# Decoder layer on one core: the samples' matrix states kept compact and turned by 64x64 products

## The chip, the cores and the metric

The kernel runs on one core of one Trainium2 chip. The metric is the device time of one execution in microseconds. The times of the kernel before are from three executions: 2606.88, 2611.5 and 2612.71 us, median 2611.5 us.

## The reference

One inference step of one layer of a hybrid decoder, for one prompt of 256 tokens and for 8 samples of 4 tokens each, all with 2048 channels. The layer normalises its input, projects it, and runs two branches side by side: a gated linear recurrence over channels, and an RWKV-7 branch with 32 heads of 64 channels. Each head has a 64x64 matrix state S (value x key). Both branches are projected back, merged, and followed by a squared-ReLU MLP and an embedding. What the change touches is the RWKV-7 state of the samples:

```
state_rwkv (DEPTH, DEC_BATCH, N_HEADS, HEAD, HEAD)   # 8 samples, 32 heads, [value, key]
sa = einsum('bhij,bhj->bhi', S, -kk_t)
S  = S * w_t[:, :, None, :] + sa[..., None] * b_t[:, :, None, :] + v_t[..., None] * k_t[:, :, None, :]
y  = einsum('bhij,bhj->bhi', S, r_t)
```

For the samples the kernel needs each state with its key index on the partitions, so every loaded 64x64 state is transposed once.

## The kernel before, in words

TensorE carries nearly everything. The large projections are cut into units: a unit is one 128-column slice of a weight against all 288 (or 296) token columns, 16 steps over the channels, three products each (high and low half of an fp32 number in two fp32r parts: `xh,wh`, `xl,wh`, `xh,wl`). SyncE loads the raw weight slice, ScalarE writes its high half `wh`, VectorE its low half `wl`, and TensorE multiplies.

The first half of the program is a loop of 16 steps, one per 128 channels, that is per pair of heads (the two heads are the two halves of 64 partitions, `head_rows(0)` and `head_rows(1)`). A step has six units, and each unit is cut into 8 slots, so a step has 48 slots. After the piece of a unit that belongs to a slot, every engine does the small stages that two tables (`EARLY` and `LATE`, line 137) put at that slot. `EARLY` belongs to the present pair of heads, `LATE` to the pair before. The order on each engine is thus written out by hand; between engines only semaphores order. Steps 0 and 1 are unrolled, steps 2 to 15 are a hardware loop, and the `LATE` stages of the last pair run beside the units of the gate projection that follows (called the last step below). What comes after (rest of the gate projection, output projections, MLP, embedding) has none of these stages.

The `LATE` stages that matter here:

- `state_in` (slot 11, lines 813 and 1168): TensorE turns the 8 sample states. The states of the two heads of a sample lie in `s0[:, b, :]` as a block-diagonal 128x128 tile whose other two blocks are zero (GpSimd clears `s0` once at the start, line 1908, first of six clears counted by `N_INIT`). `turn` (line 651) is a 128x128 transpose against the identity. The 8 results fill banks 2 and 3, and ScalarE copies each bank, 128x512, into `ms` (line 1171).
- `invert1a` to `invert5b` (slots 9 to 26): the blocks of the prompt's triangular inverse, in products of 32x32. An `a` part is 16 products into bank 6, which ScalarE copies into `yy` (line 1167); a `b` part is 16 or 32 products, which VectorE adds into `inv`. `invert2a` is at slot 12, `invert2b`, which needs the copy of `invert2a`, at slot 14.
- `samp_pair` (slot 15) writes bank 2 again and so waits for `state_read`; `samp_r` (slot 23) multiplies the turned states with `aex`, `samp_out` (slot 28) with `dg`: in both, 16 products of 64x64 with 64 columns, head 0 on rows and columns 0 to 63 of the array, head 1 on 64 to 127, by turns.
- `lowrank`, an `EARLY` stage at slot 8, writes bank 3, which ScalarE reads; the wait of `state_in` for `sig_ready` guards bank 3 against that.

SyncE loads the two heads of the next pair's states at unit 4 of a step (line 441), after the wait for `state_mm` of the pair before. `apart` (line 625) computes the value of a wait in a register ahead of the wait, where it depends on the loop counter.

All products go through one helper line (623), all transposes through line 652, so the trace tells them apart by the names of their tiles. An fp32 product has two records in the trace, a transpose one.

Of the kernel before, what the change touches and what calls it, by code (L numbers as in the profile page):

```python
# [69 lines left out]
def constants():  # L70
# [45 lines left out]

STEPS = {"dve_rg": 40, "dve_ch": 36}
ROW_LOADS = 27
N_INIT = 6
FFN_PLAN = (("up", 0), ("up", 1), ("down", 0), ("up", 2), ("down", 1), ("up", 3), ("down", 2), ("down", 3))  # L120


# [19 lines left out]
    6: ["rg_root"],  # L142
    9: ["invert1a"],
    10: ["invert1b", "rg_scan"],
    11: ["state_in"],
    12: ["invert2a"],
    14: ["invert2b"],
    15: ["samp_pair"],
    16: ["invert3a"],
# [23 lines left out]
def program(nc, a):  # L173
    ctx = ExitStack()
    with ctx:
# [31 lines left out]
        with mix:  # L207
            def mb(name, shape, dt=F32):
                return sb(name, shape, dt, mix)

            ptu, ptc = mb("ptu", [P, NPAR]), mb("ptc", [P, NPAR])
            dtc, dl = mb("dtc", [P, NDER]), mb("dl", [P, NCH])
            ex = mb("ex", [P, NX])
            zr, zk, zv = mb("zr", [P, NT]), mb("zk", [P, NT]), mb("zv", [P, NT])
            low = mb("low", [P, 4, NT])
            w2s, a2s, g2s = mb("w2s", [P, P]), mb("a2s", [P, P]), mb("g2s", [P, 2, P])
            was, wxs = mb("was", [P, P]), mb("wxs", [P, P])
            ue, xc, gg, gat = mb("ue", [P, 315]), mb("xc", [P, NT]), mb("gg", [P, NT]), mb("gat", [P, NT])
            rgi, th = mb("rgi", [P, NT]), mb("th", [P, NT])
            siga, sigw, gout, kp = (mb(n, [P, NT]) for n in ("siga", "sigw", "gout", "kp"))  # L220
            rn, ksq, kkn, bv = (mb(n, [P, NT]) for n in ("rn", "ksq", "kkn", "bv"))
            cum = mb("cum", [P, 5 * NB + NCH * (CHUNK + 1)])
            zeros = mb("zeros", [P, CHUNK])
            ar, btk = mb("ar", [P, 2, NT]), mb("btk", [P, 2, NT])
            btl, ktl = btk[:, 0, :], btk[:, 1, :]
            bkh, vv = mb("bkh", [P, 2, 2 * SAMP]), mb("vv", [P, 2, 2 * SAMP])
            tmb, tmv = mb("tmb", [P, 4, P]), mb("tmv", [P, 2, P])
            skv, suv, yts = mb("skv", [P, 2, HEAD]), mb("suv", [P, HEAD]), mb("yts", [P, HEAD])
            sbk, vpad = skv[:, 0, :], skv[:, 1, :]


            both = mb("both", [P, 9 * 4 * CHUNK])
            ams = both[:, 0:16 * CHUNK].rearrange("p (q t) -> p q t", q=4)
            am = both[:, 16 * CHUNK:16 * CHUNK + 16 * BLK].rearrange("p (l q t) -> p l q t", l=4, q=4)
            ab, yy = mb("ab", [P, 4, CHUNK]), mb("yy", [P, 4, BLK])
            inv, tt = mb("inv", [P, 8 * BLK]), mb("tt", [P, 4, CHUNK])
            tb, tn = (inv[:, k * 4 * BLK:(k + 1) * 4 * BLK].rearrange("p (q t) -> p q t", q=4) for k in range(2))
            sam, sq2, syy = mb("sam", [P, 4, SAMP]), mb("sq2", [P, 2, 2 * SAMP]), mb("syy", [P, SAMP])
            s0, ms = mb("s0", [P, NB, P]), mb("ms", [P, NB, P])
            aex, bke = mb("aex", [P, NB, 2, SAMP]), mb("bke", [P, NB, HEAD])  # L240

            dg = mb("dg", [P, NB, HEAD])
            so = dg
            rs, us, sr = mb("rs", [P, P]), mb("us", [P, P]), mb("sr", [P, HEAD])
            mp, mtmp = [mb(f"mp{k}", [P, P]) for k in range(2)], mb("mtmp", [P, P])
            sfin = mtmp
            yf, yc, ysq, sd = (mb(n, [P, NT]) for n in ("yf", "yc", "ysq", "sd"))
            dif, rgr, m2 = sd, yf, ysq
            rows = both[:, 0:D]
# [121 lines left out]
        def _(sp):  # L371
# [54 lines left out]
            def small(it, again):  # L426

                if again:
                    sp.wait_ge(cst_in, 16)
                    sp.wait_ge(bonus_mm, it)  # L430
                cols = bass.ds(it * P, P)
                sp.dma_start(g2s[:], a["rw_g2"][0, :, cols].rearrange("(k p) c -> p k c", p=P)).then_inc(small_in, 16)
                sp.dma_start(was[:], a["rg_wa"][0, bass.ds(it, 1)].rearrange("o c d -> (o c) d")).then_inc(small_in, 16)
                sp.dma_start(wxs[:], a["rg_wx"][0, bass.ds(it, 1)].rearrange("o c d -> (o c) d")).then_inc(small_in, 16)
                if again:
                    sp.wait_ge(cst_in, 16)
                    sp.wait_ge(state_mm, it)
                else:
                    sp.wait_ge(init_done, N_INIT)
                for h in range(2):  # L440
                    sp.dma_start(s0[h * HEAD:(h + 1) * HEAD, :, h * HEAD:(h + 1) * HEAD],
                                 a["state_rwkv"][0, :, bass.ds(2 * it + h, 1)].rearrange("b o i j -> (o i) b j")
                                 ).then_inc(s0_in, 16)

# [176 lines left out]
        def _(pe):  # L621
# [3 lines left out]
            def apart(value):  # L625


                if not isinstance(value, int):
                    value = pe.snap(value)
                    pe.compute_val(value)  # L630
                    pe.wait_ge(cst_in, 16)
                return value
# [18 lines left out]
            def turn(out, in_):  # L651
                return pe.transpose(out, in_, ident)  # L652
# [68 lines left out]
            def stage(name, p, last, four):  # L721
# [89 lines left out]
                                    done = mm(to(rb, 128, q), yy[rb, q, :], tn[rb, q, :], True, True)  # L811
                        done.then_inc(tn_mm, 1)
                elif name == "state_in":
                    pe.wait_ge(s0_in, 32 * one)
                    pe.wait_ge(ab_read, 2 * one)
                    if not last:
                        pe.wait_ge(sig_ready, 2 * one + 2)
                    for b in range(NB):
                        done = turn(bank[2 + b // 4][:, (b % 4) * P:(b % 4 + 1) * P], s0[:, b, :])
                    done.then_inc(state_mm, 1)  # L820
                elif name == "samp_pair":
                    count = apart(2 * one)
                    pe.wait_ge(state_read, count)
                    for h in range(2):
                        rows_h = head_rows(h)
# [20 lines left out]
                elif name == "samp_r":  # L846
# [3 lines left out]
                    for b in range(NB):  # L850
                        for h in range(2):
                            rows_h = head_rows(h)
                            mm(bank[3][rows_h, 0:HEAD], aex[rows_h, b, :, :].rearrange("p f t -> p (f t)"), ms[rows_h, b, rows_h], b == 0, False)
                    for h in range(2):
                        rows_h, rows_r = head_rows(h), slice(h * HEAD, h * HEAD + SAMP)
                        done = mm(bank[3][rows_r, 0:HEAD], sam[rows_h, 0, :], vpad[rows_h, :], False, False)
# [9 lines left out]
                elif name == "samp_out":  # L866
# [8 lines left out]
                    for b in range(NB):  # L875
                        for h in range(2):
                            rows_h = head_rows(h)
                            mm(bank[2][rows_h, b * HEAD:(b + 1) * HEAD], ms[rows_h, b, rows_h], dg[rows_h, b, :], b == 0, False)
                    for h in range(2):
                        rows_h = head_rows(h)  # L880
                        done = mm(bank[2][rows_h, :], suv[rows_h, :], bke[rows_h, :, :], False, True)
# [180 lines left out]
        def _(act):  # L1062
# [71 lines left out]
            def stage(name, p):  # L1134
# [32 lines left out]
                    act.activation(yy[:].rearrange("p a b -> p (a b)"), bank[6][:, 256:256 + 4 * BLK], ACT.Copy).then_inc(yy_read[int(name[6]) - 1], 1)  # L1167
                elif name == "state_in":
                    act.wait_ge(state_mm, one)
                    for b in range(2):  # L1170
                        act.activation(ms[:, 4 * b:4 * b + 4, :].rearrange("p a b -> p (a b)"), bank[2 + b][:], ACT.Copy).then_inc(state_read, 1)
                elif name == "samp_inv_a":
                    act.wait_ge(syy_mm, one)
                    act.activation(syy[:], bank[3][:, 0:SAMP], ACT.Copy).then_inc(syy_read, 1)
# [727 lines left out]
        @block.gpsimd  # L1902
        def _(pool):
            pool.memset(rows[0:NPAR, :], 0.0).then_inc(rows_zero, 1)

            pool.wait_ge(par_ready, 2)
            pool.wait_ge(nrm_lo, 8)
            for view, value in ((s0[:], 0.0), (cum[:], 1.0), (zeros[:], 0.0), (ue[:], 0.0), (sq2[:], 0.0), (vv[:], 0.0)):
                pool.memset(view, value).then_inc(init_done, 1)

            def samples(p):


                pool.wait_ge(am_ready, p + 1)
                if not (isinstance(p, int) and p == 0):
                    pool.wait_ge(so_saved, 16 * p)
                pool.tensor_tensor(aex[:], ar[:, :, samp_all].unsqueeze(1).to_broadcast([P, NB, 2, SAMP]),
                                   cst[:, C_SEQ:C_SEQ + 256].rearrange("p (b t) -> p b t", b=NB).unsqueeze(2).to_broadcast([P, NB, 2, SAMP]), ALU.mult)
                pool.tensor_tensor(dg[:], cst[:, C_ID2:C_ID2 + HEAD].unsqueeze(1).to_broadcast([P, NB, HEAD]),
                                   cum[:, NS * NB:(NS + 1) * NB].unsqueeze(2).to_broadcast([P, NB, HEAD]), ALU.mult)  # L1920
                pool.wait_ge(turn_read, p + 1)
                ins = pool.tensor_tensor(bke[:], sbk.unsqueeze(1).to_broadcast([P, NB, HEAD]),
                                         cst[:, C_SQT:C_SQT + NB].unsqueeze(2).to_broadcast([P, NB, HEAD]), ALU.mult)
                ins.then_inc(sexp_ready, 1)

            samples(0)
            with pool.Fori(1, KT) as p:
                samples(p)
# [30 lines left out]
```

## Time and profile before

| what | us |
|---|---|
| median of three executions | 2611.5 |
| the profiled execution | 2610.33 |
| span of its profile | 2608.6 |
| TensorE busy in the span | 2527.0 (97%) |
| VectorE busy | 1550.0 (59%) |
| ScalarE busy | 1114.7 (43%) |
| GpSimd busy | 62.8 (2%) |

The span is what the profile shows from the first to the last instruction; 1.7 us of the execution lie outside it. PE is TensorE's matmul side, PEld its weight loads, DVE VectorE, ACT ScalarE, POOL GpSimd. Matmuls overlap: the duration of one contains its way through the array, so the time that a block of them takes is read from the start of its first to the start of what follows it.

### The profile page before, as it was taken

How to read it: one execution, taken by the hardware profiler on the slowest of the kernel's cores; microseconds unless marked ns; L12 is line 12 of the kernel's file. 1: busy time of each engine (PE TensorE's matmuls, PEld its weight loads, DVE VectorE, ACT ScalarE, POOL GpSimd, SP SyncE). 2: the span in 40 equal slices, each digit the busy share in tenths (PEclk: the TensorE clock that was granted, in tenths of full speed). 3: DMA queues.
4: the chain of work that ended last, by engine and by line, in shares of the span. 5: the costliest groups of instructions: out<-in, count | busy, mean ns of one | idle time of the engine just before them, and what ended most of it. 6: DMA issues, size and time to landing. Idle time of an engine off the chain costs nothing.

```text
span 2608.6 us, 66543 instructions
## 1 busy us (share of the span) xinstructions
PE 2527.0 (97%) x27452; PEld 2368.5 (91%) x27452; DVE 1550.0 (59%) x2818; ACT 1114.7 (43%) x1514; POOL 62.8 (2%) x59
## 2 busy tenths in 40 slices
PE   5999999999999999998999999999999999999997
PEld 4988888888888888887999999999999999999996
DVE  5667776776676766774444566555444444446665
ACT  3545555555554544453433333444334324333333
POOL 0000000000000000000000000000000000000000
PEclk8999999999999999998999999999999999999998
DMA  5643434443434434343567665556655655665553
GB/s 159 156 109 101 113 93 115 103 109 100 113 97 115 115 99 115 97 111 96 138 188 224 184 184 161 162 164 167 168 161 163 175 161 161 168 166 164 158 152 93
DMA packets 699783, 363.59 MB, mean 139 GB/s; under 512 B 43905, under 2 KB 698531, under 8 KB 698659
## 3 DMA queue, kind: packets, MB, share of 16 engines
q1 hardware_dynamic: 699598, 360.70, 51.3%
q8 instruction: 168, 2.75, 0.5%
q14 instruction: 17, 0.14, 0.0%
HBM read 346.07 MB, written 14.59 MB: 138 GB/s over the span
## 4 chain that ended last, share of the span: by engine, by line
PE 90%; DVE 5%; DMA 1%; issue 1%; ACT 1%; DVEq 0%; SPq 0%; ACTq 0%
PE bank L623 89%; DVE sd L1710 1%; PE bank L652 1%; DVE yc L1380 1%; DMA raw<-w_in 1%; DVE wl L1722 1%; DVE nrm L1380 0%; ACT ysq L1197 0%; DMA gb_scratch<-gat 0%; DVE bv L1380 0%; DVE sd L1383 0%; DVE wl L1374 0%; ACT sd L1200 0%; DMA nsq<-ga_scratch 0%; DVE xl L1377 0%
## 5 line engine op out<-in xcount | busy, mean ns | idle before, releaser
L623 PE MATMUL bank<-xh,wh 128*128 128x288 f32 (+1 forms) x3136 | 1002.1, 320 | 17.8 <-DVE xl L1377 10.4
L623 PE MATMUL bank<-xh,wl 128*128 128x288 f32 (+1 forms) x3136 | 932.4, 297 | 0.9 <-issue 0.9
L623 PE MATMUL bank<-xl,wh 128*128 128x288 f32 (+1 forms) x3136 | 932.7, 297 | 0.0
L623 PEld LDWEIGHTS bank<-xh,wh 128*128 128x128 f32 x3136 | 593.9, 189 | 54.7 <-issue 16.3
L1374 DVE TENSOR_TENSOR wl<-raw,wh 128x2048 fp32r<-128x2048 f32 x206 | 472.1, 2292 | 232.5 <-ACT wh L1068 232.5
L623 PEld LDWEIGHTS bank<-xl,wh 128*128 128x128 f32 x3136 | 595.1, 190 | 6.0
L623 PEld LDWEIGHTS bank<-xh,wl 128*128 128x128 f32 x3136 | 594.5, 190 | 1.1 <-issue 1.1
L623 PE MATMUL bank<-sbh,wl 128*128 128x288 f32 x1792 | 534.0, 298 | 0.0
L623 PE MATMUL bank<-sbh,wh 128*128 128x288 f32 x1792 | 529.6, 296 | 1.8 <-DVE wl L1374 1.8
L623 PE MATMUL bank<-sbl,wh 128*128 128x288 f32 x1792 | 529.5, 295 | 0.0
L1068 ACT ACTIVATE wh<-raw 128x2048 fp32r<-128x2048 f32 x206 | 392.6, 1906 | 285.6 <-PE bank L623 276.4
L623 PEld LDWEIGHTS bank<-sbh,wh 128*128 128x128 f32 x1792 | 336.7, 188 | 2.1 <-issue 2.1
L623 PEld LDWEIGHTS bank<-sbl,wh 128*128 128x128 f32 x1792 | 338.4, 189 | 0.0
L623 PEld LDWEIGHTS bank<-sbh,wl 128*128 128x128 f32 x1792 | 336.7, 188 | 0.0
L1722 DVE TENSOR_TENSOR wl<-raw,wh 128x1024 fp32r<-128x1024 f32 x204 | 241.6, 1219 | 5.1 <-ACT wh L1234 4.2
L1234 ACT ACTIVATE wh<-raw 128x1024 fp32r<-128x1024 f32 x204 | 212.8, 1053 | 47.7 <-PE bank L623 47.3
L1329 ACT ACTIVATE tmp<-tmp 128x288 f32<-128x288 f32 x64 | 28.5, 445 | 225.3 <-DVE tmp L1380 225.3
L1377 DVE TENSOR_TENSOR rga<-rga,bank 128x288 f32 (+1 forms) x80 | 36.4, 454 | 145.1 <-PE bank L623 145.1
L1686 DVE COPY us<-bank 64x128 f32<-64x128 f32 x64 | 18.5, 289 | 141.8 <-PE bank L623 141.8
L1189 ACT ACTIVATE rs<-bank 64x128 f32<-64x128 f32 x64 | 17.4, 272 | 139.2 <-PE bank L623 139.2
L1377 DVE TENSOR_TENSOR sbl<-tmp,sbh 128x288 f32 (+1 forms) x64 | 29.3, 459 | 77.1 <-ACT sbh L1331 77.1
L1317 ACT ACTIVATE xh<-rga,par 128x288 fp32r<-128x288 f32 x32 | 17.2, 537 | 130.2 <-DVE rga L1377 130.2
(282 smaller groups left out, 2400.9 us busy)
## 6 DMA issues: line engine op xcount, KB each, us to landing
raw<-w_in SPq DMA_DIRECT2D x116, 1024.0 KB, 5.9
raw<-w_up SPq DMA_DIRECT2D x64, 1024.0 KB, 6.3
raw<-w_down SPq DMA_DIRECT2D x64, 1024.0 KB, 5.9
raw<-w_rg_o SPq DMA_DIRECT2D x16, 1024.0 KB, 6.0
raw<-w_rw_o SPq DMA_DIRECT2D x16, 1024.0 KB, 6.0
raw<-w_o SPq DMA_DIRECT2D x16, 1024.0 KB, 6.0
raw<-w_ple_gate SPq DMA_DIRECT2D x16, 1024.0 KB, 6.0
s<-state_rwkv SPq DMA_DIRECT2D x32, 128.0 KB, 4.2
```

The source lines that it names most:

```text
L623: return pe.matmul(out, lhsT, rhs, start=start, stop=stop, skip_group_check=True)
L652: return pe.transpose(out, in_, ident)
L1068: act.activation(wh[slot][:], raw[slot][:], ACT.Copy).then_inc(hi_done, 1)
L1189: act.activation(rs[rc, :], bank[4][rc, g * P:(g + 1) * P], ACT.Copy).then_inc(r_read[c], 1)
L1234: act.activation(wh[slot][:, k, :], raw[slot][:, k, :], ACT.Copy).then_inc((half_done, hi_done)[part], 1)
L1329: act.activation(tmp[u][:], tmp[u][:], ACT.Square).then_inc(h_sq, 1)
L1374: dve.tensor_tensor(wl[slot][:], raw[slot][:], wh[slot][:].bitcast(F32), ALU.subtract).then_inc(lo_done, 1)
L1377: return dve.tensor_tensor(out, x, y, op)
L1380: return dve.scalar_tensor_tensor(out, x, s, y, op0, op1)
L1686: dve.tensor_copy(us[rc, :], bank[5][rc, 0:P]).then_inc(u_read, 1)
L1710: dve.reciprocal(sd[:], sd[:]).then_inc(ch.sem, ch.one())
L1722: ins = dve.tensor_tensor(wl[slot][:, k, :], raw[slot][:, k, :], wh[slot][:, k, :].bitcast(F32), ALU.subtract)
```

## The change

The states are kept as 64 columns a sample instead of 128, with head 0 on partitions 0 to 63 and head 1 on 64 to 127 and no zero blocks. Each state is turned by a product with the 64x64 identity (`C_ID2` of the constants), which makes 16 products on 64x64 parts of the array instead of 8 transposes on the whole. The result is one bank (2) instead of two, copied once. The stage stands in slot 12 behind `invert2a` instead of in slot 11. The wait for `sig_ready` is gone since bank 3 is no longer written, and the other two waits take their values through `apart`. GpSimd's clear of `s0` is gone, so five clears are counted. The readers of `ms` address it without the head's column offset.

```diff
-N_INIT = 6
+N_INIT = 5
-    11: ["state_in"],
-    12: ["invert2a"],
+    12: ["invert2a", "state_in"],
-            s0, ms = mb("s0", [P, NB, P]), mb("ms", [P, NB, P])
+            s0, ms = mb("s0", [P, NB, HEAD]), mb("ms", [P, NB, HEAD])
@@ SyncE, small()
-                    sp.dma_start(s0[h * HEAD:(h + 1) * HEAD, :, h * HEAD:(h + 1) * HEAD],
+                    sp.dma_start(s0[h * HEAD:(h + 1) * HEAD, :, :],
@@ TensorE, state_in
-                    pe.wait_ge(s0_in, 32 * one)
-                    pe.wait_ge(ab_read, 2 * one)
-                    if not last:
-                        pe.wait_ge(sig_ready, 2 * one + 2)
+                    count = apart(32 * one)
+                    pe.wait_ge(s0_in, count)
+                    count = apart(2 * one)
+                    pe.wait_ge(ab_read, count)
                     for b in range(NB):
-                        done = turn(bank[2 + b // 4][:, (b % 4) * P:(b % 4 + 1) * P], s0[:, b, :])
+                        for h in range(2):
+                            rows_h = head_rows(h)
+                            done = mm(bank[2][rows_h, b * HEAD:(b + 1) * HEAD], s0[rows_h, b, :], cst[rows_h, C_ID2:C_ID2 + HEAD], True, True)
@@ TensorE, samp_pair
-                    count = apart(2 * one)
+                    count = apart(one)
                     pe.wait_ge(state_read, count)
@@ TensorE, samp_r (and in samp_out the same edit of ms)
-... ms[rows_h, b, rows_h] ...
+... ms[rows_h, b, :] ...
@@ ScalarE, state_in
-                    for b in range(2):
-                        act.activation(ms[:, 4 * b:4 * b + 4, :].rearrange("p a b -> p (a b)"), bank[2 + b][:], ACT.Copy).then_inc(state_read, 1)
+                    act.activation(ms[:].rearrange("p a b -> p (a b)"), bank[2][:], ACT.Copy).then_inc(state_read, 1)
@@ GpSimd
-            for view, value in ((s0[:], 0.0), (cum[:], 1.0), (zeros[:], 0.0), (ue[:], 0.0), (sq2[:], 0.0), (vv[:], 0.0)):
+            for view, value in ((cum[:], 1.0), (zeros[:], 0.0), (ue[:], 0.0), (sq2[:], 0.0), (vv[:], 0.0)):
```

## Rows read from the trace of the kernel before

**Rows 1.** The page, first part: busy time, share of the span, instructions.
```profile
PE 2527.0 (97%) x27452; PEld 2368.5 (91%) x27452; DVE 1550.0 (59%) x2818; ACT 1114.7 (43%) x1514; POOL 62.8 (2%) x59
```

**Rows 2.** TensorE's waits in the loop: total us, times, longest.
```profile
PE bank L623 <- ACT yy L1167: 7.4, 2, 4.1
PE bank L623 <- ACT rs L1189: 7.1, 16, 0.5
```

**Rows 3.** Timeline of TensorE, slots 11 and 12 of one step: start, length.
```profile
704.78 0.30 PE L623 MATMUL bank<-xh,wl 128*128 128x296 f32 x1
704.91 1.03 PE L652 MATMUL bank<-cst,s 128*128 128x128 f32 x8
705.71 0.38 PE L623 MATMUL bank<-xh,wh 128*128 128x296 f32 x1
705.92 0.29 PE L623 MATMUL bank<-xl,wh 128*128 128x296 f32 x1
...
706.47 0.30 PE L623 MATMUL bank<-xh,wl 128*128 128x296 f32 x1
706.70 0.45 PE L623 MATMUL bank<-inv,both 32*32 32x32 f32 x32
707.08 0.40 PE L623 MATMUL bank<-xh,wh 128*128 128x296 f32 x1
707.32 0.30 PE L623 MATMUL bank<-xl,wh 128*128 128x296 f32 x1
```

**Rows 4.** The chain of waits over the loop: start us, us, what.
```profile
634.70 0.87 PE bank L652 x8
...
705.08 0.87 PE bank L652 x8
...
1207.24 7.16 DMA gb_scratch<-gat
```

**Rows 5.** Timeline of TensorE, samp_out and r0 of the same step.
```profile
728.84 1.15 PE L623 MATMUL bank<-dg,ms 64*64 64x64 f32 x32
729.82 1.03 PE L623 MATMUL bank<-bke,suv 64*64 64x512 f32 x4
730.68 0.25 PE L623 MATMUL bank<-cst,yts 64*64 64x32 f32 x4
730.77 0.66 PE L623 MATMUL bank<-tmv,both 64*64 64x64 f32 x16
```

**Rows 6.** Timeline of TensorE, samp_u and invert5b, then my0.
```profile
726.17 0.33 PE L623 MATMUL bank<-sr,sq 32*64 32x64 f32 x4
726.43 0.21 PE L623 MATMUL bank<-yy,inv 32*32 32x32 f32 x1
...
734.51 0.33 PE L623 MATMUL bank<-us,tmb 64*64 64x64 f32 x4
734.68 0.28 PE L623 MATMUL bank<-tmv,tmb 64*64 64x64 f32 x4
734.79 0.33 PE L623 MATMUL bank<-both,us 64*64 64x64 f32 x4
```

**Rows 7.** Timeline of ScalarE, the same step.
```profile
705.99 1.09 ACT L1171 ACTIVATE ms<-bank 128x512 f32<-128x512 f32 x2 [1.48 <-PE bank L652]
...
707.53 1.28 ACT L1130 ACT_TABLE_LOAD   x1
...
711.61 0.45 ACT L1132 ACTIVATE rn<-rn 128x288 f32<-128x288 f32 x1 [1.04 <-DVE rn L1383]
```

**Rows 8.** Timelines of TensorE: a hiccup in the loop; the last step.
```profile
225.85 0.24 PE L623 MATMUL bank<-inv,both 32*32 32x32 f32 x2 [0.42 <-issue]
...
1216.08 0.65 PE L623 MATMUL bank<-yy,inv 32*32 32x32 f32 x32 [3.34 <-ACT yy L1167]
```

**Rows 9.** The states' tile s: the clear, and the load's issue-to-landing.
```profile
L1909 POOL MEMSET s<- x1: 955/955/955, 56.2 to 56.2; 128x1024 f32 x1
DMA to landing us min/median/max: 3.8/4.2/4.9
```

More of the change, by code:

```diff
@@ L852, in stage @@
                             rows_h = head_rows(h)
-                            mm(bank[3][rows_h, 0:HEAD], aex[rows_h, b, :, :].rearrange("p f t -> p (f t)"), ms[rows_h, b, rows_h], b == 0, False)
+                            mm(bank[3][rows_h, 0:HEAD], aex[rows_h, b, :, :].rearrange("p f t -> p (f t)"), ms[rows_h, b, :], b == 0, False)
                     for h in range(2):
@@ L877, in stage @@
                             rows_h = head_rows(h)
-                            mm(bank[2][rows_h, b * HEAD:(b + 1) * HEAD], ms[rows_h, b, rows_h], dg[rows_h, b, :], b == 0, False)
+                            mm(bank[2][rows_h, b * HEAD:(b + 1) * HEAD], ms[rows_h, b, :], dg[rows_h, b, :], b == 0, False)
                     for h in range(2):
```

## The prediction, made before the changed kernel was run

> **What bounds the kernel.** I read the page's first part first: TensorE is busy for 2527.0 of 2608.6 us, 97%, and no other engine reaches 60% [rows 1]. An edit pays only by what it takes off TensorE's queue, or by a wait of TensorE that it shortens. The second view was therefore TensorE's own waits in the loop of 16 steps. Two matter: 16 waits of at most 0.5 us for ScalarE's `rs` at slot 34, which `state_in` does not feed, and two long ones, together 7.4 us, for the copy `yy` [rows 2]. Both long ones lie in the last step, where ScalarE stands behind the store of a gate (below). In the 14 steps of the hardware loop TensorE goes through slots 9 to 28 nearly without a pause, so there a nanosecond of its work is a nanosecond of the run. A step takes 70.38 us, from one `state_in` to the next (634.70 to 705.08) [rows 4].
>
> The third view was the timeline of slots 11 and 12. From 705.92 to 706.47 there are four intervals between large products, 0.137 us each. The 8 transposes start at 704.91, the next large product at 705.71 and the one after at 705.92 [rows 3]. From 704.78 to 705.92 are 1.14 us, where two intervals of 0.137 would have stood: the transposes cost 0.87 us. The chain of waits gives the same figure, 0.87, for this step, and it has 15 such pieces at `state_in`'s place, one a step, all of 0.87, of which two stand in the rows; only the last step's is missing [rows 4].
>
> **The change, part by part.**
>
> *TensorE, removed:* 8 transposes and their place in slot 11, -0.87 us a step.
>
> *TensorE, added:* 16 fp32 products, each with 64 rows, 64 columns of weights and 64 moving columns, the heads by turns on opposite quarters of the array, 32 records. The trace has exactly this shape: the `dg,ms` block of `samp_out`. Its 32 records start at 728.84, and the next block of the same shape of array starts at 729.82 [rows 5]: 0.98 us, 31 ns a record. That a product accumulates there and starts afresh here is no difference that I price. Nearest rows on both sides: 4 records of `us,tmb` take 0.17 us, 42 ns each, and 4 of `tmv,tmb` 0.11 us, 27 ns each [rows 6]. Bounds for the block are so 0.88 and 1.36 us; I take 0.98, because that row is the same pattern at the same length.
>
> *TensorE, the company it keeps.* A block on parts of the array pays for the change of shape. Into `invert2a` the distance from start to start is 0.23 us instead of 0.14 (706.47, 706.70), and behind it the first large product takes 0.24 (707.08, 707.32) [rows 3]; the end of the block itself also hides a gap. Its size between small shapes: 4 records of 64x32 followed by the same shape of array take 0.09 us (730.68, 730.77) [rows 5], 4 records of 32x64 followed by 32x32 take 0.26 (726.17, 726.43) [rows 6]. The difference, 0.17 us, is what I charge for going from 32x32 to 64x64 inside slot 12. Entry from and return to the large shape are already paid by `invert2a`; that is what the new place saves. The bounds of this term: 0, if the change of shape hides behind the last 32x32 products, and 0.17.
>
> Sum for a step: -0.87 + 0.98 + 0.17 = +0.28 us. By the low bounds it is -0.87 + 0.88 + 0 = +0.01, by the high ones -0.87 + 1.36 + 0.17 = +0.66.
>
> The Trainium skill ("TensorEngine Tiling (Array Packing)", Performance Considerations, Instruction Overhead) says that each matmul bears about 60 cycles of overhead on this chip, which speaks against 16 short products in place of 8 long ones. If that were paid on top of the columns by each of the 32 records, it would be, as an estimate from that page at 2.4 GHz, 25 ns more a record and 0.8 us more a step. The `dg,ms` row, 31 ns a record in all, leaves no room for it; where it came from, some of it would be in the 42 ns of `us,tmb`.
>
> *How many steps count.* Fifteen: the unrolled first one, 14 in the loop. In the last step TensorE does not set the pace: the chain goes through a store of the gate, `gb_scratch<-gat`, from 1207.24 for 7.16 us [rows 4], and TensorE sits idle for 3.34 us until 1216.08 behind it [rows 8]. The store is released by VectorE, which waits for nothing of `state_in`, so 0.28 us more is swallowed there, and a cheaper `state_in` would not have helped either. Sum: 15 x 0.28 = +4.2 us; bounds +0.2 and +9.9.
>
> *The waits.* The states are issued in unit 4 of the step before and land in 4.2 us [rows 9], with more than 10 slots to spare before they are used. `ab_read` is done at slot 6. `sig_ready` gone: the transposes started 0.13 us behind the product before them [rows 3], so none of the three waits cost anything, and nothing is gained by dropping one. The two `apart` are instructions of TensorE's queue and not of its array. `invert2a`, which has one, enters 0.09 us late in all [rows 3], and most of that is the change of shape; for two behind 32 queued records I take zero, at most 0.09. Queued behind the new block's waits are the large products of slot 13, which wait for nothing more, since both semaphores rose several slots before.
>
> *ScalarE.* The copies took 1.09 us together, from 705.99 on [rows 7]; one takes half, 0.5 to 0.6. But it now comes after the `yy` copy. With slot 11 empty everything starts 0.87 earlier: `yy` is copied about 706.4 to 706.7, the turning ends about 707.3, the copy runs to about 707.95, and the table load that stood at 707.53 starts 0.4 us later. Behind it `rn` waits 1.04 us for VectorE anyway [rows 7], so the delay is swallowed. `invert2b` needs `yy` only at slot 14, 2 us on, and `samp_pair` needs the copy at slot 15, about 3 us later. Gain and cost zero. Without that cover, 0.4 us a step would be 6 us.
>
> *VectorE* does nothing for `state_in`. *SyncE* issues the same two loads with the same 256-byte pieces in memory; its wait for `state_mm` comes at unit 4, 20 slots after the turning: zero. *GpSimd* loses a clear of 0.96 us at 56.2 [rows 9]; those that ask for the clears do so in the first step's own slots, much later: zero, and 0.96 us at the most if one had waited. The readers of `ms` fetch the same 64 contiguous numbers: zero.
>
> The profiled execution took 2610.33 us and its span 2608.6; with 4.2 more, 2614.5 and 2612.8. Its time is 1.2 us under the median of the three, so for the median I predict 2611.5 + 4.2 = 2615.7, rounded to 2615.5 us. Three executions spread over 5.8 us, and about 0.2%, 5.2 us, is what can be told from no change.
>
> **The rivals.**
>
> *A. Each short product costs more than the twin row says* (slower). 32 weight loads of 64x64 in place of 8 of 128x128, each hidden only behind 64 columns. For it: the 42 ns of `us,tmb` [rows 6]. Against it: that is a block of four with nothing to pipeline, the long block shows 31. Price 15 x 0.66 = +9.9 us, 2621. It decides from +0.35 us a step (5.2 us over 15 steps): block and switch together over 1.22 us, or 33 ns a record with the switch at 0.17.
>
> *B. TensorE's instruction supply* (slower). The step gets 48 more instructions (64 loads and products for 16) in the densest part of the queue. In some steps TensorE already halts for 0.42 us in the middle of a block of 32x32 products with nothing but issue to blame, at 225.85 and in four other steps [rows 8]. If all 15 steps halt once, that is ten more halts, +4.2 on top of 4.2: 2620. Equally the boundary can move to a harmless place, which takes back 2.1 us: 2613.5; that is within my forecast.
>
> *C. ScalarE's relief counts* (faster). If the 0.5 us a step that ScalarE saves came back on TensorE, the sum would be 4.2 - 7.5 = -3.3 us, 2608; with the low bounds for the products, 0.2 - 7.5 = -7.3, 2604. For it: ScalarE is the one for whom TensorE waits in the loop [rows 2]. Against it: that wait is at slot 34, 22 slots on, and ScalarE is idle before `rn` [rows 7].
>
> *D. It does nothing:* products at 27 ns and a hidden switch, +0.2 us, 2611.7. It is the low end of my own sum.
>
> **How the numbers follow.** Forecast with D as its low end, +0 to +6 us: 0.62. A 0.13, B 0.12, C 0.13. Of the forecast's 0.62 I leave 0.07 to more than +5.2 us (upper part of the terms, and the spread of three runs). Slower by over 0.2%: 0.07 + 0.13 + 0.12 = 0.32. Faster by over 0.2%: 0.08, the better part of C. Within: 0.60. The range goes from 2609 (C's milder case nearly) to 2621 (A): it leaves out part of C and what lies beyond A, together under 0.2.
>
> **What would show it.** Right: in slot 12 a block `cst,s` of 32 records, 0.95 to 1.15 us to the next large product after its 32x32 neighbour, no block in slot 11; the distance of one step to the next 70.6 to 70.7 us where it was 70.37; one copy `ms` of about 0.6 us after `yy`; TensorE's waits for `rs` unchanged at 0.45. Wrong: a block of 1.3 us or more (A), more halts with issue alone in slots 9 to 21 (B), steps under 70.3 us (C), or a time that moved outside the loop, between 0 and 110 us or after 1290, where I expect the same numbers.

## The result: slower, and by more than the sum allowed

The changed kernel takes 2627.06 us in the median of four executions (2623.62 to 2628.96), the kernel before 2609.19 us in the same four: ratio 1.0062, 95% interval [1.0044, 1.0081]. That is 16 to 18 us, where I had forecast +4.2 and a range that ended at 2621. One of the ten executions of e9 below ran at a granted clock of 0.41 and took 6036 us; the time of e9 is the median of the other nine. The profiled execution took 2625.82 us, its span is 2624.0 us, 15.4 over the 2608.6 of before.

The page of the changed kernel, first part, for [rows 1]:

```profile
span 2624.0 us, 67308 instructions
## 1 busy us (share of the span) xinstructions
PE 2528.6 (96%) x27836; PEld 2368.1 (90%) x27836; DVE 1550.7 (59%) x2818; ACT 1107.4 (42%) x1498; POOL 61.8 (2%) x58
```

TensorE is busy for 1.6 us more than before and the span is 15.4 us longer: what was added is nearly all idle time. TensorE's waits over 13 steps of the loop, 190 to 1180 us, first of the changed kernel, then of the kernel before (total us, times, longest; the rows of [rows 2] are of a longer stretch):

```profile
PE bank L622 <- issue: 17.5, 12, 1.8
PE bank L622 <- ACT rs L1189: 6.3, 14, 0.5
...
PE bank L623 <- issue: 2.7, 9, 0.4
PE bank L623 <- ACT rs L1189: 6.4, 14, 0.5
```

The waits for ScalarE are what they were. The first line is new in size: 12 halts with "issue", in which TensorE waited for nothing that the profile shows. They all sit at one place. TensorE's timeline of two steps of the changed kernel, at the halt, and at slot 12, where the states are turned:

```profile
291.86 0.30 PE L622 MATMUL bank<-xh,wh 128*128 128x296 f32 x1
293.66 0.30 PE L622 MATMUL bank<-xl,wh 128*128 128x296 f32 x1 [1.50 <-issue]
293.80 0.30 PE L622 MATMUL bank<-xh,wl 128*128 128x296 f32 x1
...
710.71 0.30 PE L622 MATMUL bank<-xh,wl 128*128 128x296 f32 x1
710.93 0.45 PE L622 MATMUL bank<-inv,both 32*32 32x32 f32 x32
711.35 1.15 PE L622 MATMUL bank<-cst,s 64*64 64x64 f32 x32
712.43 0.40 PE L622 MATMUL bank<-xh,wh 128*128 128x296 f32 x1
712.66 0.30 PE L622 MATMUL bank<-xl,wh 128*128 128x296 f32 x1
```

The halt stands between two large products of one unit in slot 19 (the expectations below say near slot 20), which wait for no semaphore: 10 us behind the new block, in the middle of plain work. The block itself runs as the twin row said. From the 32x32 products to the first `cst,s` are 0.42 us (0.38 to the large product in [rows 3]), from there to the next large product 1.08 us: 1.12 us added, where I had 0.98 + 0.17 = 1.15.

What is late at the halt is TensorE's own program. The instructions come from memory over the DMA rings, the queues that carry the weights too. The DMA view of the changed kernel, in 40 slices of a window: above a step that halts (291 to 292 us), below one that does not (359 to 360.5 us). The row `q8 instruction` counts fetches of instructions, in pieces of 16 KB; the spike in the GB/s row is the fetch.

```profile
DMA  9999999999999999999999999999999999998999
GB/s 266 881 307 225 266 287 266 287 266 328 225 266 246 287 246 307 287 266 307 246 287 307 266 266 287 307 287 307 266 348 307 246 307 287 246 374 225 333 272 354
q8 instruction: 1, 0.02, 7.4%
...
DMA  0000000000000000000000090000113667494573
GB/s 0 0 0 0 0 0 0 0 0 0 0 0 0 0 0 0 0 0 0 0 0 0 0 437 0 0 0 0 55 41 123 164 150 177 123 150 137 164 164 109
q8 instruction: 1, 0.02, 4.0%
```

In the good step the piece is fetched at 359.9 on empty rings, 0.2 us before a weight load begins. In the halting step the rings are full for the whole window: the load has been on them since 288, the fetch starts at 291.0, takes 1.2 us, and TensorE goes on at 293.66. Counted from the bonus product of slot 2 (`bv,cst`), the same fetch starts at 19.4 to 19.5 us in the two good steps and at 22.1 to 23.1 in the 12 that halt; the load runs from about 19.5 to 24. When TensorE asks for a piece, the trace does not show.

One interval is nearly the same everywhere. In every halt of 0.3 us or more in the hardware loop, in all runs of this document, TensorE goes on 2.2 to 2.8 us after the fetch has started. So a halt is as long as those 2.2 to 2.8 us, less the work that TensorE still has when the fetch starts.

This was my rival B, with the wrong size and place. Two theories for the experiments, then. **Supply by position:** where the instructions stand against the 16 KB pieces decides when TensorE asks for the next piece, and a fetch that meets a weight load starts some 3 us late. **The products:** the halts come from the new block itself, its number of instructions or its place.

### The profile page after: what moved, and what is told of

Read it like the earlier page. It is cut to its first block, busy times and chain, and to the rows that moved or that the text cites. A ratio compares the mean times of both kernels' runs of the same rounds, so it can differ in the third digit from the quotient of the medians.

```text
span 2624.0 us, 67308 instructions
## 1 busy us (share of the span) xinstructions
PE 2528.6 (96%) x27836; PEld 2368.1 (90%) x27836; DVE 1550.7 (59%) x2818; ACT 1107.4 (42%) x1498; POOL 61.8 (2%) x58
## 4 chain that ended last, share of the span: by engine, by line
PE 87%; DVE 6%; DMA 2%; issue 2%; ACT 1%; SPq 0%; DVEq 0%; ACTq 0%
PE bank L622 87%; DVE sd L1710 1%; DMA gb_scratch<-gat 1%; DVE wl L1722 1%; DVE yc L1380 1%; DMA raw<-w_in 1%; PE bank L651 0%; DVE nrm L1380 0%; DVE bv L1380 0%; DMA nsq<-ga_scratch 0%; DVE sd L1383 0%; DVE wl L1374 0%; ACT ysq L1197 0%; ACT sd L1200 0%; ACT wh L1234 0%
## 5 line engine op out<-in xcount | busy, mean ns | idle before, releaser
L622 PE MATMUL bank<-xl,wh 128*128 128x288 f32 (+1 forms) x3136 | 931.4, 297 | 17.5 <-issue 17.5
L1377 DVE TENSOR_TENSOR inv<-inv,bank 128x256 f32<-128x256 f32 x64 | 26.8, 419 | 89.9 <-PE bank L622 82.4
```

The source lines that it names most:

```text
L622: return pe.matmul(out, lhsT, rhs, start=start, stop=stop, skip_group_check=True)
L1377: return dve.tensor_tensor(out, x, y, op)
```

## Experiments

Each was run in three rounds with the kernel before beside it. A "shift" puts small 32x32 products on a free bank, once, before the loop: 4 instructions each, and everything behind them moves in memory. They take 1.5 us (24 of them, e2) to 3.8 us (60, e13) before 22 us, and in every run the bonus product of the second step starts at 197 to 200 us. How many instructions a piece holds I took to be about 256: a step has some 2190, and 9 or 10 fetches.

**e1: 48 more instructions in the step, nothing of the change.**

```diff
-                                for rb in blocks:
+                                for rb in blocks * (2 if l == 2 and q < 3 else 1):
                                     done = mm(to(rb, 256, q), am[rb, l - 1, q, :], tb[rb, q, :], True, True)
```

> The kernel before; 12 of the 16 products of invert2a are issued twice in every step (same operands, same place in bank 6), which adds 48 instructions (24 weight loads, 24 products) to TensorE's queue in slot 12 and nothing else. If the halts of the changed kernel come from TensorE's instruction supply, they appear here too: halts of 1 to 2 us with nothing but issue to blame, near slot 20, in most steps, and 12 to 22 us over before. If they come from the 64x64 products of the turned states or their place, this costs only its own 0.2 to 0.3 us a step: +3 to +5 us, no halt over 0.5 us.

Measured: 2611.89 us, ratio 1.0008 [0.9999, 1.0018]. Its waits:

```profile
PE bank L623 <- issue: 5.7, 4, 1.7
```

These are four halts of 1.2 to 1.7 us at slot 19, in 4 steps; the others had none. So the halts appear without any turned state, but far fewer than I expected: the number of instructions alone is not what decides. Nor is the position alone: e1's instructions stand where those of the changed kernel stand, and that one halts in 12 steps. In e1's good steps the fetch starts at 18.4 to 19.9 us, in the four others at 22.5 to 22.9: it either gets ahead of the load or does not, and by these times a fraction of a microsecond decides.

**e2: the loop untouched, 96 instructions of shift.**

```diff
             pe.wait_ge(xt_dve, 4)
+            for _ in range(24):
+                mm(bank[6][0:BLK, 0:BLK], cst[0:BLK, C_EYE:C_EYE + BLK], cst[0:BLK, C_EYE:C_EYE + BLK], True, True)
```

> The kernel before, its loop untouched; 24 small products on a free bank are issued once near the start, so that everything behind them on TensorE stands 96 instructions further on in memory: as far as what follows slot 12 of the loop does in the changed kernel. If it is the position of the instructions against the pieces in which they are fetched (16 KB) that makes the halts, they appear here: +10 to +20 us. If it is the number of instructions in a step, nothing changes here beyond 0.5 us at the start: within 2 us of before.

Measured: 2626.57 us, ratio 1.0073 [1.0054, 1.0091]: the whole loss of the change, from a loop in which not one instruction differs. TensorE's waits and one halt in e2:

```profile
PE bank L623 <- issue: 13.7, 8, 1.9
...
223.13 0.30 PE L623 MATMUL bank<-xl,wh 128*128 128x296 f32 x1
224.88 0.30 PE L623 MATMUL bank<-xh,wl 128*128 128x296 f32 x1 [1.45 <-issue]
```

The halt is at the same unit and slot as in the changed kernel. (The profiled execution, with its 8 halts, is the fastest of the four, 2618.68 us.)

**e3: the changed kernel with 160 instructions of shift** (40 products in the same place). The change moved what follows slot 12 by 96, so with 160 more it is 256 from where it stood before, one piece if a piece holds 256.

> The changed kernel; 40 small products are issued once near the start, so that what follows slot 12 of the loop stands 256 instructions from where it stood in the kernel before, that is at the same place in its 16 KB piece. By position: the halts near slot 20 go, and the time is before + 3 to 6 us (the terms of my sum). By number of instructions in the step, or by the products themselves: the halts stay, before + 14 to 18 us.

Measured: 2608.68 us, ratio 0.9996 [0.9987, 1.0006]. The halts are gone:

```profile
PE bank L622 <- issue: 0.2, 1, 0.2
```

Its fetches behind slot 12 start nearly where those of the kernel before do (the fourth at 23.2 to 23.9 us in both), as a piece of 256 would have it. The time is even under the +3 to +6 that I expected, because most of the small halts of the kernel before [rows 8] went too. The changed kernel is level with the kernel before when its instructions stand well; its own 0.25 us a step is still there (e8, e9 and e11 below).

**e4: transposes and two copies as before, but in slot 12 behind `invert2a`.**

> The kernel before with its 8 transposes of 128x128 and its two copies, but in slot 12 behind invert2a instead of in slot 11. The number of instructions is that of before. Instruction supply: no halt over 0.5 us, and the two places cost alike, within 2 us of before. If the place in slot 12 is what costs (something late behind the copies, or a drain), then halts or waits appear here: +10 us or more.

Measured: 2608.49 us, ratio 0.9998 [0.9989, 1.0008]. The place costs nothing that can be told. The small halts stay, 3.6 us in 11 of them, the longest of 0.6 us a little over what I expected.

**e5: e2 with a weight load cut, the wrong one.** The unit's load is cut for u == 2; e9 to e11 have the same edit with u == 1.

```diff
-                        load_unit(in_columns(unit_columns(u + 3, it)), (u + 3) % 2, n)
+                        load_unit(in_columns(unit_columns(u + 3, it)), (u + 3) % 2, n, 2 if u == 2 else KT)
```

> The kernel before, 96 instructions shifted as in e2 (which ran 17 us over before, with halts of 1.5 to 2 us near slot 20 in 9 of 15 steps), and one weight load a step is cut: that of the sixth unit, which starts at slot 20, fetches 2 of its 16 blocks of rows (the other 14 keep old numbers, so part of the first gate is computed from wrong weights). If the halts come from the instruction fetch standing behind this load in the DMA rings, they go: before - 4 to + 2 us. If the fetch is late at this position whatever the rings do, they stay: +10 to +18 us.

Measured: 2619.96 us, ratio 1.0032 [1.0012, 1.0052], 8 halts. My expectation placed the load wrongly: the one I cut starts at 29 us into the step, and the one on the rings from 19 to 24 is that of the fifth unit. As a test of the theory this run says nothing against it, since the load in question was still there. Whether the load that follows matters is not settled: the traces of e5 and e2 have 8 halts each (14.4 and 13.7 us), with the fetch at 22.2 to 23.2 us in e5's, but the median of e5 is 6.6 us under that of e2, and e5's executions range from 2608.75 to 2623.08, e2's from 2618.68 to 2631.98.

**e9, e10, e11: the fifth unit's load cut**, in the changed kernel, in e2, and in the kernel before as the control.

> The changed kernel; the weight load of the fifth unit of each step, the one that is on the wire from 19 to 24 us into the step, fetches 2 of its 16 blocks of rows (the gate of the recurrent branch is computed from partly wrong weights). e5 cut the load behind it, at 29 us, and the halts stayed. If the late instruction fetch is late because it stands behind this load, the halts go: 10 to 18 us under the changed kernel, so before -3 to +6. If it is late by itself: before + 14 to 18 us.

> e2 (the kernel before, shifted by 96 instructions, 17 us over before) with the same load cut to 2 of 16 blocks (part of the gate computed from wrong weights). Fetch behind the load: no halts over 0.5 us, a step of 70.0 us, before - 6 to 0. Fetch late by itself: before + 10 to 17 us.

> The kernel before, unshifted, with the same load cut to 2 of 16 blocks (part of the gate computed from wrong weights): the control of e9 and e10. Fetch behind the load: the small halts of 0.3 to 0.6 us before the last two products of invert4a go too, a step of 70.0 to 70.1 us in place of 70.4, before - 3 to - 6 us. If not: level with before.

Measured: e9 2606.68 us, ratio 0.9992 [0.9982, 1.0002]; e10 2602.17 us, 0.9970 [0.9959, 0.9981]; e11 2604.37 us, 0.9980 [0.9970, 0.9990]. All three as the fetch behind the load has it, e10 even 1.5 us below its range. The load fell from 1024 to 128 KB, and with that e9 is some 20 us under the changed kernel and e10 some 24 us under e2. The fetch itself moved: it starts at 18.7 to 21.2 us in e9 (22.1 to 23.1 in the halting steps of the changed kernel), at 18.3 to 21.2 in e10 (22.4 to 22.9 in those of e2), and at 20.7 to 21.3 in e11 (23.3 to 23.9 in the kernel before). TensorE's waits over 13 steps of the loop (190 to 1180 us) of e9 have no line with issue at all:

```profile
PE bank L622 <- ACT rs L1189: 6.3, 14, 0.5
PE bank L622 <- ACT ysq L1197: 3.6, 15, 0.2
PE bank L622 <- DVE bv L1380: 0.2, 1, 0.2
```

With no halts at slots 19 to 21 on either side, e9 against e11 is the change by itself: 2.3 us in the medians, each known to about 2.6 us, and in their steps 70.27 to 70.45 against 70.01 to 70.08 us. The 14 steps of the loop grow by 2.8 us (981.6 to 984.4), and e11 has one halt, of 0.8 us, where the loop is left (1178 us), that e9 lacks: 3.9 us without it, 0.28 a step.

**e6: the products alone in slot 11**, shifted as e3.

> The changed kernel with the shift of e3 (160 instructions, which ran level with before), but the turning by 64x64 products back in slot 11 by itself. By my term for the change of shape, leaving the company of invert2a costs another entry and return, 0.2 to 0.33 us a step: +3 to +5 us over e3. If a change of shape costs nothing to speak of: within 1 us of e3. No halts of over 0.5 us in either case.

Measured: 2608.74 us, ratio 0.9993 [0.9983, 1.0002]: level with e3, and not the 3 to 5 us over it that my term for the change of shape asked for. TensorE's timeline of e6 at slot 11:

```profile
703.75 0.30 PE L623 MATMUL bank<-xh,wl 128*128 128x296 f32 x1
703.97 1.15 PE L623 MATMUL bank<-cst,s 64*64 64x64 f32 x32
705.05 0.41 PE L623 MATMUL bank<-xh,wh 128*128 128x296 f32 x1
705.29 0.30 PE L623 MATMUL bank<-xl,wh 128*128 128x296 f32 x1
```

1.54 us where two intervals of 0.137 would stand: 1.27 us alone against 1.12 in company. The company of `invert2a` saves 0.15 us a step, half of what I had thought; the steps differ by 0.1 us, too little to see in the time.

**e7 and e8: the loop of the kernel before, shifted by 160 and by 208.**

> The kernel before, its loop untouched, shifted by 160 instructions. In e2 (shift 96) the fetch that collides was asked for about 18.5 us into the step in the good steps and stood behind the weight load that starts at 21 us in the bad ones; 64 instructions further it is asked for 1 to 2 us earlier, always ahead of the load. By position and rings: no halts over 0.5 us, a step of about 70.0 us instead of 70.4, so 3 to 6 us under before. If a shift merely moves the halt elsewhere: +5 us or more.

> The kernel before, its loop untouched, shifted by 208 instructions, that is 48 back from the next whole piece of 256. The collision then comes later in TensorE's queue than in before, behind the dense blocks: by position and rings either level with before or up to 5 us under it, and not over +3. If every shift away from zero costs: +5 us or more.

Measured: e7 2642.9 us, ratio 1.0121 [1.0104, 1.0137]; e8 2603.35 us, 0.9975 [0.9965, 0.9984]. e8 beats both kernels with an untouched loop, 7 us under before where I expected up to 5; its steps take 70.00 to 70.07 us. Its fetch starts at 23.6 to 24.4 us, behind the load as in the kernel before, and still no step halts: a late fetch costs something only where TensorE needs its instructions soon. e7 missed by 37 us: slot 19 was clean, but the halt came back elsewhere. Its waits, and one of them; then the granted clock (the number before the last two) of 2 us before it and 2 us behind it; then the same place where the loop is left, at 1219 us:

```profile
PE bank L623 <- issue: 35.3, 13, 3.5
...
264.10 0.27 PE L652 MATMUL bank<-cst,vv 128*128 128x128 f32 x1
266.90 0.86 PE L623 MATMUL bank<-xc,was 128*128 128x288 f32 x2 [2.53 <-issue]
...
262.00:264.00 2.00, 2.00 (x19) 2.00 (x18) 1.49 (x2) 1.90 (x3) 0.00 (x0) 1.00 1.18 312
268.80:270.80 2.00, 2.00 (x10) 2.00 (x10) 0.86 (x3) 1.83 (x3) 0.00 (x0) 0.50 0.00 0
...
1219.44 0.27 PE L652 MATMUL bank<-cst,vv 128*128 128x128 f32 x1
1219.55 0.65 PE L623 MATMUL bank<-xc,was 128*128 128x288 f32 x2
```

`xc,was` is `rg_gates`, slot 0, right behind the jump back to the loop's start. There e7 has two fetches 3.4 to 4.1 us apart, at 66 us, as a weight load that runs from 62 to 67 goes out, and at 70; TensorE halts before and during the first. e8 has the fetch at 66 alone and does not halt. e7 halts at each of its 13 jumps, and when the loop is left, where no jump is taken, it runs from `cst,vv` to `xc,was` in 0.11 us, with the same load on the rings. That points to the jump, though what follows the loop also stands elsewhere in memory. Whether the load plays any part there no run tests.

The halt has a second price. In 7 of the 13 steps of e7 the granted clock was 0.50 (the 1.2 GHz level) for some microseconds after TensorE had stood, and large products came every 0.25 us in place of 0.137. Those steps take 73.9 to 74.9 us, the other six 72.4 to 72.7. In e12 it is 10 steps of 13, in e14 7, in the loops of the kernel before, e8 and e13 none.

**e12: a version to beat both.** Shift 208, `state_in` in slot 12 as in e4, and half of the last `tn` products left away, whose result nothing reads.

```diff
-                                for rb in blocks:
+                                for rb in blocks if l < 4 else blocks[0::2]:
                                     done = mm(to(rb, 128, q), yy[rb, q, :], tn[rb, q, :], True, True)
```

> A version to beat both: the kernel before with the shift of e8 (208 instructions, 0.25% under before), its transposes in slot 12 as in e4, and without the products of invert4b that renew the odd blocks of tn, which nothing reads afterwards (8 products of 32x32, 32 instructions a step, 0.14 us). If positions are as harmless here as in e8: 2 us under e8, 7 to 10 us under before. If 32 instructions fewer behind slot 22 bring a fetch behind a load again: between before and + 15 us.

Measured: 2656.25 us, ratio 1.0192 [1.0172, 1.0211]: less work, and the slowest of all. Issue waits of 43.0 us in 13 steps, all behind the jump back. The edit also shortens the unrolled steps ahead of the loop by 32 instructions, so the loop began 176 on, next to e7's 160, and not 208.

**e13 and e14: where the loop begins.** e13 is e12 with 60 products in place of 52; e14 is the changed kernel with 28, so that its loop begins where that of e7 does.

> e12 with 240 instead of 208 instructions of shift. The unrolled steps of e12 lost 32 instructions, so its loop began where it begins in e7 (shift 160) within 16 instructions, and both halt for 2.6 to 3.6 us right behind the jump back, with two fetches 3.8 us apart there. With 240 the loop begins where it does in e8, which had no halt. By position of the loop's start: a step of 69.9 us, 7 to 10 us under before. If leaving out the products is to blame for e12: it stays over before + 20.

> The changed kernel with 112 instructions of shift: its loop then begins where it begins in e7 (48 of its own unrolled step and 112), the rest of it 48 further. By position of the loop's start: halts of 2.5 us or more behind the jump back in nearly every step, 20 to 45 us over before, though the halts near slot 20 are gone. If the halts behind the jump back belong to the loop of the kernel before alone: within 6 us of before.

Measured: e13 2602.67 us, ratio 0.9971 [0.9960, 0.9982], no issue waits; e14 2647.94 us, 1.0143 [1.0123, 1.0164], and in its waits

```profile
PE bank L622 <- issue: 31.2, 13, 2.7
```

Both as expected. e13 is 54 us faster than e12 by 32 instructions that run once. Against e8 its own saving does not show in the time: 2602.67 against 2603.35, and their intervals overlap. In the traces the 14 steps of the loop take 979.4 against 980.4 us.

| kernel | loop begins | ratio to before | issue waits, 13 steps |
|---|---|---|---|
| before | 0 | 1 | 2.7 us |
| changed | 48 | 1.0062 | 17.5 |
| e1 | 48 | 1.0008 | 5.7 |
| e2 | 96 | 1.0073 | 13.7 |
| e7, e14 | 160 | 1.0121, 1.0143 | 35.3, 31.2 |
| e12 | 176 | 1.0192 | 43.0 |
| e3 (changed) | 208 | 0.9996 | 0.2 |
| e8, e13 | 208 | 0.9975, 0.9971 | 0 |

("Loop begins" is my count of instructions added ahead of it. In the changed kernel and its variants e3 and e14, and in e1, 48 more lie inside the loop at slot 12. The issue waits are those of the one profiled execution, 190 to 1180 us.)

## Why the prediction was wrong

*What bounds the kernel* held: TensorE's queue is the run. But I wrote that in slots 9 to 28 it goes "nearly without a pause" and took for granted that the queue is always filled. [rows 8] showed a halt with issue alone; it was the visible end of the thing.

*The sum* held term by term, as far as it went. Removed 0.87 us, added 1.12 (I had 1.15): +0.25 us a step for my +0.28. The pair of controls, e9 and e11, gives 2.3 us in the medians and 3.9 in the loop for my 4.2; e3 against e8, whose loops begin at the same place, gives 5.3, of which some 2.5 are small halts and the halt on leaving the loop, which e8 has not. The stretch behind the loop is no longer than before, so the last step swallowed its share as far as the trace can tell, and the switch of shape costs about what I charged, though a slot of its own is only 0.15 us dearer, not the 0.2 to 0.33 of e6's expectation.

*The step that failed* is rival B's price and its chance; in the sum itself TensorE's instruction supply stood at nothing. I knew of 48 more instructions in the step and costed a halt at the 0.42 us of [rows 8], ten of them, with 0.12 of chance, as if a halt had a fixed size. It measured 0.8 to 1.8 us of wait, in 12 steps: 17.5 us. From start to start, against the shortest step, these halts are 19.5 us and those of before 5.2 us, so 14.2 us more; with 14 steps of 0.25 us that is 17.7, and the 14 steps of the hardware loop grew by 17.5 (986.5 to 1004.0 us from bonus product to bonus product). Two smaller things nearly cancel in it: after the last halt of 1.84 us the granted clock was 0.50 from 1155 to 1159 us, which cost 1.3 us (24.1 us from slot 13 to slot 28, against 22.8 in a step with the same halt), and the kernel before halts for 0.86 us where the loop is left (1184 us), which the changed one does not. The span as a whole grew by 2.1 less, since the stretches before and after the loop were that much shorter in this execution. Nor was the number of instructions the cause, as I had put it: e2 has the whole loss with none added to the loop. It is their position, together with how soon TensorE needs the piece whose fetch meets the load (e2, e8, e9 to e11).

*ScalarE* did as written: a single copy of 0.60 us behind `yy`, the table load after it, nothing late. The timeline of ScalarE in the changed kernel, for [rows 7]:

```profile
711.46 0.28 ACT L1168 ACTIVATE yy<-bank 128x128 f32<-128x128 f32 x1 [1.83 <-PE bank L622]
712.53 0.60 ACT L1171 ACTIVATE ms<-bank 128x512 f32<-128x512 f32 x1 [0.79 <-PE bank L622]
713.15 1.28 ACT L1131 ACT_TABLE_LOAD   x1
```

*Rival A* is out: block and switch together took 1.12 us, under the 1.22 from which it would have decided. *Rival C* is out: TensorE's wait for `rs` is still 0.45 us, with 16 copies fewer.

Why the halts behind the jump back are longer follows from the 2.2 to 2.8 us: at slot 19 of the changed kernel TensorE still works for 0.7 to 1.8 us after the fetch has started, while behind the jump back it runs out at about the fetch's start in e7 and e14 and 0.7 to 1.1 us before it in e12. What stays open: how far ahead TensorE asks, and why the loop's start is not at hand after the jump in e7, e12 and e14 but is in the others, which fetch at 66 us too. That the load is needed is shown only for slot 19 (and for the small halts at slot 21, by e11). Behind the jump back the position is shown to matter (e7, e12, e13, e14); that the jump does is likely from e7's way out of the loop, and that the load does is not shown.

## What to carry to other kernels

Where TensorE runs a long loop body and large loads are on the DMA rings, its instruction fetches are a transfer like any other: look in the waits for issue alone, place the fetches against the loads, and before a small edit is called slower, run it once more with a few dozen instructions put ahead of the loop. Here the position alone was worth from -0.25% to +1.2% with an untouched loop (e8, e7), and 2.1% between e13 and e12, more than any edit of the work in this study, so a change of 0.2% cannot be judged at one position. To price an edit by itself, compare both kernels where neither halts. A halt can also lower the clock of the work behind it, so read the granted clock there before its cost is put down to the wait alone.

## What was not expected of the hardware

- A 16 KB instruction fetch that meets a 1 MB weight load started about 3 us later than one that just preceded it (22.1 to 23.1 against 19.5 us into the step), and TensorE then stood for 0.8 to 1.8 us; with the load cut to 128 KB no step halted there. In every halt of 0.3 us or more in the loops TensorE went on 2.2 to 2.8 us after the fetch's start.
- Right behind a loop's jump back TensorE stood for up to 3.5 us a step, when the loop begins where e7, e12 and e14 have it; a second fetch then follows the first within about 4 us. After 24 of these 39 halts the granted clock was 0.50 for a while: with the same halt of 2.42 us a step of e7 took 73.9 us where that happened and 72.4 us where it did not.
- A few dozen 32x32 products on an idle bank, issued once near the start, moved the time of a 2610 us program between 2603.35 us (e8) and 2642.9 us (e7).
- For the same data, each in a slot of its own and less the two intervals that would stand there anyway, 8 fp32 transposes of 128x128 cost 0.87 us and 16 products of 64x64 on two opposite quarters of the array 1.27 us (e6): the transposes are the cheaper way.
